# Two-block transformer kernel: the gated product turned by VectorE in squares of 32 instead of by TensorE

## What is computed

```
def swiglu(x, w_gate, w_up, w_down):
    return (jax.nn.silu(x @ w_gate) * (x @ w_up)) @ w_down

h = h + 0.5 * swiglu(rms_norm(h, norm_ffn), w_gate, w_up, w_down)   # eight times, 1024 -> 2816 -> 1024
```

## Time and profile before

| | us |
|---|---|
| median of 3 runs | 1971.68 (1971.55 to 1972.51) |
| the profiled execution, its own time | 1972.77 |
| its span in the profile | 1971.0 |
| TensorE busy in the span | 1960.5 |
| VectorE busy | 1199.4 |
| ScalarE busy | 1018.6 |

### The profile page before, as it was taken

How to read it: one execution, slowest core, us unless ns; L and a number is a source line. 1 busy time by engine, 2 the same in 40 slices (tenths; PEclk the granted TensorE clock), 3 DMA queues, 4 the chain that set the end, 5 groups by cost and what they waited for, 6 DMA issues and landing times.

```text
span 1971.0 us, 26229 instructions
## 1 busy us (share of the span) xinstructions
PE 1960.5 (99%) x9838; PEld 1652.8 (84%) x9838; DVE 1199.4 (61%) x1817; ACT 1018.6 (52%) x1590; POOL 68.9 (3%) x77
## 2 busy tenths in 40 slices
PE   9999999999999999999999999999999999999999
PEld 7888988888888898888888898888888888888887
DVE  6555656556655566555755566655576555876554
ACT  6444555445554665444544447544475444755442
POOL 0100300000000000000000000000010000200000
PEclk9999999999999999999999999999999999999999
DMA  9655436553655426555555434555446553306550
GB/s 339 210 202 174 150 108 214 192 191 130 221 184 178 144 77 212 192 192 171 188 181 186 162 138 139 203 192 192 171 163 234 183 189 128 108 24 212 192 192 22
DMA packets 241050, 338.91 MB, mean 172 GB/s; under 512 B 5728, under 2 KB 206351, under 8 KB 240831
## 3 DMA queue, kind: packets, MB, share of 16 engines
q1 hardware_dynamic: 239710, 335.84, 50.5%
q0 software_dynamic: 496, 1.23, 0.2%
q10 hardware_dynamic: 752, 0.61, 0.1%
HBM read 336.61 MB, written 1.05 MB: 171 GB/s over the span
## 4 chain that ended last, share of the span: by engine, by line
PE 95%; DVE 2%; ACT 2%; DMA 1%; issue 0%; SPq 0%; POOL 0%; ACTq 0%
PE A L535 11%; PE A L537 11%; PE A L536 11%; PE G L535 10%; PE G L537 10%; PE G L536 10%; PE X L535 8%; PE X L537 8%; PE X L536 8%; PE A L1226 1%; PE A L904 1%; PE G L964 1%; PE X L964 1%; PE X L1210 1%; PE G L1238 1%; DVE wl L496 0%
## 5 line engine op out<-in xcount | busy, mean ns | idle before, releaser
L496 DVE TENSOR_TENSOR wl<-raw,wh 128x1024 fp32r<-128x1024 f32 (+1 forms) x553 | 653.8, 1221 | 121.3 <-ACT wh L487 120.3
L487 ACT ACTIVATE wh<-raw 128x1024 fp32r<-128x1024 f32 (+1 forms) x553 | 561.9, 1058 | 144.1 <-PE A L537 102.6
L535 PE MATMUL G<-wh,xh 128*128 128x512 f32 (+1 forms) x814 | 322.1, 396 | 0.2
L537 PE MATMUL G<-wh,xl 128*128 128x512 f32 (+1 forms) x814 | 317.2, 390 | 0.0
L536 PE MATMUL G<-wl,xh 128*128 128x512 f32 (+1 forms) x814 | 316.3, 389 | 0.0
L535 PE MATMUL X<-wh,xh 128*128 128x512 f32 x672 | 265.8, 395 | 0.3 <-DVE wl L496 0.3
L537 PE MATMUL X<-wh,xl 128*128 128x512 f32 x672 | 262.3, 390 | 0.0
L536 PE MATMUL X<-wl,xh 128*128 128x512 f32 x672 | 261.6, 389 | 0.0
L537 PEld LDWEIGHTS G<-wh,xl 128*128 128x128 f32 x814 | 152.8, 188 | 32.3
L535 PEld LDWEIGHTS G<-wh,xh 128*128 128x128 f32 x814 | 152.9, 188 | 30.9 <-DVE xl L2399 0.6
L536 PEld LDWEIGHTS G<-wl,xh 128*128 128x128 f32 x814 | 153.1, 188 | 29.9
(11 more groups left out here) (487 smaller groups left out, 2787.5 us busy)
## 6 DMA issues: line engine op xcount, KB each, us to landing
raw<-in_ffn_w_in SPq DMA_DIRECT2D x88, 1024.0 KB, 6.8
raw<-in_ffn_w_down SPq DMA_DIRECT2D x44, 1024.0 KB, 6.5
raw<-in_ffn_w_out SPq DMA_DIRECT2D x44, 1024.0 KB, 7.1
raw<-in_ffn_w_gate SPq DMA_DIRECT2D x42, 1024.0 KB, 5.5
raw<-in_ffn_w_up SPq DMA_DIRECT2D x42, 1024.0 KB, 7.5
raw<-in_a_w_in SPq DMA_DIRECT2D x12, 1024.0 KB, 6.1
raw<-in_ab_w_in SPq DMA_DIRECT2D x8, 1024.0 KB, 6.8
raw<-in_kv_w SPq DMA_DIRECT2D x6, 1024.0 KB, 6.5
```

The lines of the kernel that those rows point to most:

```text
L487: nc.scalar.activation(hi, r, ACT.Copy).then_inc(hi_done[u], 1)
L496: nc.vector.tensor_tensor(lo, r, hi.bitcast(F32), ALU.subtract).then_inc(lo_done[u], 1)
L535: nc.tensor.matmul(o, sh, rh, start=start, stop=False)
L537: return nc.tensor.matmul(o, sl, rh, start=False, stop=stop)
```

## The change

`turn_hid` goes out of TensorE's step for the blocks 0 to 9 of each phase. In its place VectorE's `turn_squares` turns the product in SBUF, right behind `hidden`: a VectorE transpose turns squares of 32 by 32. Sixteen of them, one for each pair of input and output groups of 32 partitions, put each square in its place of the 128 by 128 transpose; each takes the squares of both token tiles and both halves of the 256 columns at once. `hid_hi` and `hid_lo` then read SBUF (`hid_t`) in place of PSUM. The last block of each phase is still turned by TensorE (`turn_hid`, `last_hid_hi`, `last_hid_lo`). ScalarE computes Silu in one pass, so `hidden` has one product per token tile in place of two, and `rstd2` is gone. Four events of the mixers are merged into two, with the counts moved accordingly.

```diff
@@ TensorE
-                def turn_hid(b, turn=None):
-                    at = 0 if turn is None else 4 * turn
+                def turn_hid(b):
                     for t in range(NT):
-                        pe.wait_ge(hid_done, 2 * (FFN_BLOCKS * f + b) + t + 1 + at)
+                        pe.wait_ge(hid_done, 2 * (FFN_BLOCKS * f + b) + t + 1)
...
                 def step(b, turn=None):
                     gate_up(b, 0, turn)
-                    turn_hid(b - 1, turn)
                     gate_up(b, 1, turn)
                     down(b - 1, turn)
...
                 gate_up(end, 0)
-                turn_hid(end - 1)
                 gate_up(end, 1)
@@ ScalarE
-                        A_(sig[:, t, :], GB[b % 2][t][:, 0:S], ACT.Sigmoid, scale=rstd[:, t:t + 1]).then_inc(sig_ready, 1)
+                        A_(sig[:, t, :], GB[b % 2][t][:, 0:S], ACT.Silu, scale=rstd[:, t:t + 1]).then_inc(sig_ready, 1)
...
                 def hid_hi(b, turn=None):
-                    at = 0 if turn is None else 4 * turn
+                    at = 0 if turn is None else 2 * turn
+                    act.wait_ge(squares_turned, (FFN_BLOCKS - 1) * f + b + 1 + at)
                     for t in range(NT):
-                        act.wait_ge(hid_turned, 2 * (FFN_BLOCKS * f + b) + t + 1 + at)
+                        A_(hidh[:, b % 2, t * S:(t + 1) * S], hid_t[:, t, :], ACT.Copy).then_inc(hidh_done, 1)
+
+                def last_hid_hi():
+                    b = FFN_BLOCKS - 1
+                    for t in range(NT):
+                        act.wait_ge(hid_turned, 2 * f + t + 1)
                         A_(hidh[:, b % 2, t * S:(t + 1) * S], GB[b % 2][t][:, 0:S], ACT.Copy).then_inc(hidh_done, 1)
...
             act.wait_ge(dve_chain, 1)
-            A_(zinv[:, 0:1], y[:, 0, 0:1], ACT.Sigmoid)
+            A_(zinv[:, 0:1], y[:, 0, 0:1], ACT.Silu)
@@ VectorE
                         dve.wait_ge(sig_ready, n + t + 1)
-                        V.tensor_tensor(gated[:, t, :], GB[b % 2][t][:, 0:S], sig[:, t, :], ALU.mult).then_inc(gated_done, 1)
-                    for t in range(NT):
-                        dve.wait_ge(gated_done, n + t + 1)
-                        V.scalar_tensor_tensor(hid[:, t, :], GB[b % 2][t][:, S:2 * S], rstd2[:, t:t + 1], gated[:, t, :],
+                        V.scalar_tensor_tensor(hid[:, t, :], GB[b % 2][t][:, S:2 * S], rstd[:, t:t + 1], sig[:, t, :],
                                                ALU.mult, ALU.mult).then_inc(hid_done, 1)
+
+                def turn_squares(b, turn=None):
+
+                    at = 0 if turn is None else 4 * turn
+                    dve.wait_ge(hid_done, 2 * (FFN_BLOCKS * f + b) + 2 + at)
+                    for q in range(4):
+                        for g in range(4):
+                            src = hid[32 * q:32 * (q + 1), :, :].rearrange("p t (c g j) -> p t c g j", c=2, g=4)
+                            dst = hid_t[32 * g:32 * (g + 1), :, :].rearrange("p t (c q j) -> p t c q j", c=2, q=4)
+                            last = V.transpose(dst[:, :, :, q, :], src[:, :, :, g, :])
+                    last.then_inc(squares_turned, 1)
...
                     hidden(b - 1, turn)
+                    turn_squares(b - 1, turn)
                     for half in downs:
                         prep(name, half, (2,))
                     for u in (0, 1):
...
-                link(V.tensor_tensor(rstd2, rstd, rstd, ALU.mult))
```

More of the change, by code:

```diff
@@ L346, in blocks_program @@
         mhf, mlf = mh[:].rearrange("p c n -> p (c n)"), ml[:].rearrange("p c n -> p (c n)")
-        sumsq, meansq, rstd, rstd2 = stat(2), stat(2), stat(2), stat(2)
+        sumsq, meansq, rstd = stat(2), stat(2), stat(2)
         zinv = stat(4)
@@ L354, in blocks_program @@
         sig = cut(work, 0, 2, S)
-        gated, hid = cut(work, 2 * S, 2, S), cut(work, 4 * S, 2, S)
+        hid = cut(work, 2 * S, 2, S)
+        hid_t = cut(work, 4 * S, 2, S)
         PT = cut(work, 0, 2, TRI)
@@ L375, in blocks_program @@
         xhi_done, xlo_done, acc_done = sem("xhi_done"), sem("xlo_done"), sem("acc_done")
-        sig_ready, gated_done, hid_done = sem("sig_ready"), sem("gated_done"), sem("hid_done")
+        sig_ready, hid_done = sem("sig_ready"), sem("hid_done")
+        squares_turned = sem("squares_turned")
         hid_turned, hidh_done, hidl_done = sem("hid_turned"), sem("hidh_done"), sem("hidl_done")
@@ L1861, in ffn @@
                     prep(name, FT + 1, (0, 1))
-                hid_hi(FFN_BLOCKS - 1)
+                last_hid_hi()
             def start(name):
@@ L1954, in fox_mixer @@
                 link(A_(fox["e"], fox["nz"], ACT.Exp))
-                A_(fox["e"], fox["e"], ACT.Ln, bias=1.0).then_inc(event("fox_ln"), 1)
+                A_(fox["e"], fox["e"], ACT.Ln, bias=1.0).then_inc(event("gate_ln"), 1)
                 for g in range(4):
@@ L1961, in fox_mixer @@
                     last = A_(decay[at:at + FOX_H, :], A[3][at:at + FOX_H, 0:S], ACT.Copy, scale=-1.0)
-                last.then_inc(event("fox_sums_hi"), 1)
+                last.then_inc(event("gate_hi"), 1)
                 wait_half(act, "fox", *ROWS["fox"][1][:2])
@@ L2067, in mlstm_mixer @@
                 link(A_(mls["e"], mls["nz"], ACT.Exp))
-                A_(mls["e"], mls["e"], ACT.Ln, bias=1.0).then_inc(event("ml_ln"), 1)
+                A_(mls["e"], mls["e"], ACT.Ln, bias=1.0).then_inc(event("gate_ln"), 1)
                 prep("mlstm", 3)
@@ L2072, in mlstm_mixer @@
                     last = A_(decay[at:at + ML_H, :], mls["top"][at:at + ML_H, 0, P:], ACT.Copy, scale=-1.0)
-                last.then_inc(event("ml_top_hi"), 1)
+                last.then_inc(event("gate_hi"), 1)
                 def gates(chunks):
@@ L2460, in hid_lo, with last_hid_lo @@
                         dve.wait_ge(hidh_done, 2 * (FFN_BLOCKS * f + b) + t + 1 + at)
+                        part = slice(t * S, (t + 1) * S)
+                        V.tensor_tensor(hidl[:, b % 2, part], hid_t[:, t, :], hidh[:, b % 2, part].bitcast(F32),
+                                        ALU.subtract).then_inc(hidl_done, 1)
+                def last_hid_lo():
+                    b = FFN_BLOCKS - 1
+                    for t in range(NT):
+                        dve.wait_ge(hidh_done, 2 * (FFN_BLOCKS * f + b) + t + 1)
                         part = slice(t * S, (t + 1) * S)
@@ L2527, in ffn @@
                     prep(name, FT + 1, (0, 1))
-                hid_lo(FFN_BLOCKS - 1)
+                last_hid_lo()
                 if name == "ffn0":
@@ L2650, in fox_mixer @@
                 split_keys(1)
-                dve.wait_ge(event("fox_ln"), 1)
+                dve.wait_ge(event("gate_ln"), 1)
                 V.scalar_tensor_tensor(fox["logf"], fox["z"], 0.0, fox["e"], ALU.min, ALU.subtract
@@ L2658, in fox_mixer @@
                                            ).then_inc(o_lo, 1)
-                dve.wait_ge(event("fox_sums_hi"), 1)
+                dve.wait_ge(event("gate_hi"), 1)
                 V.scalar_tensor_tensor(decay[32:40, :], A[3][32:40, 0:S], -1.0, decay[32:40, :].bitcast(F32),
@@ L2801, in mlstm_mixer @@
                 prep("mlstm", 2)
-                dve.wait_ge(event("ml_ln"), 1)
+                dve.wait_ge(event("gate_ln"), 2)
                 V.scalar_tensor_tensor(mls["logf"], z[:, :, 8:16], 0.0, mls["e"], ALU.min, ALU.subtract
@@ L2830, in mlstm_mixer @@
                                 ).then_inc(event("ml_top_out"), 1)
-                dve.wait_ge(event("ml_top_hi"), 1)
+                dve.wait_ge(event("gate_hi"), 2)
                 V.scalar_tensor_tensor(decay[32:40, :], top[32:40, 0, P:], -1.0, decay[32:40, :].bitcast(F32), ALU.mult,
```

## The result

The changed kernel takes 1981.57 us (median of 5 runs, 1980.83 to 1984.31); the kernel before took 1972.28 beside it on the same chip (5 runs, 1971.55 to 1973.58). The ratio is 1.005, with a 95% interval of 1.0035 to 1.0064: **slower by 9.3 us**, about 0.5%. The forecast was 1971.2, no difference. The time lies inside the range, but the chance for slower was 0.37, and the likeliest case was another one.

A forecast was written before the change was run, and what follows sets the result against it. TensorE, busy 1960.5 of 1971.0 us, was taken as the bound. Transposes saved (-38.4), waits (+36.6) and a table load (+1.3) summed to -0.5 us: 1972.3 in the profiled execution, 1971.2 as median; range 1954 to 1986.

The forecast's parts named there:

- Granted clock 1.00 after each wait: Expected sign in the trace: TensorE keeps its full granted clock after every wait at a phase start.
- The granted clock falls in the waits: Rival: 1.2 GHz for half a block after each of eight waits, +43 us at most, half giving 1993; chance 0.08.
- TensorE's gain: Each of 80 blocks loses TensorE's four transposes, 0.48 us each time, 38.4 us off.
- The transposes: On VectorE, one transpose takes p = 0.33 us without overlap; T, the time of all sixteen, is 5.28 us.
- overlap: Rival: VectorE transposes in a row overlap, 0.20 to 0.23 us each, -20 to -15 us, 1952 to 1957; chance 0.11.
- a slow element and of VectorE as the bound: Rival: two cycles per 4-byte element, 0.43 us per transpose, make VectorE bound every block, 1993 us; chance 0.10.
- the one that named 1980: Rival: each VectorE transpose takes between 0.36 and 0.42 us, +5 to +14 us, 1980 us; chance 0.10.
- The waits: TensorE's lateness at eight phase starts and ffn2's block 3: 9T - 11.34 + 0.4 = 36.6 us.
- ffn6: Second half of block 1: TensorE late by T - 1.26 us; kv's second table load falls in ScalarE's idle time, free.
- ffn2, block 3: After the rotary tables' angles: TensorE late by T - 2.48, plus about 0.4 us for a later last hidl.
- The kv load ahead of the gates: ScalarE needs one new table load before the kv stage's Sigmoid gates, on the chain, +1.3 us.
- the middle blocks inside their cover: In the other blocks VectorE's residuals come 4.7 us later, within 6.34 us before TensorE needs them: no cost.

The follow-up runs named there:

- the filled kernel: Changed kernel plus TensorE matmuls whose results nobody reads, placed where TensorE would wait at the phase starts: 1967.13 us, ratio 0.9973 to the kernel before.
- the kernel without waits: Changed kernel, but block 0 of each phase is turned by TensorE as before, the other nine by VectorE: 1937.59 us, ratio 0.9822.
- kernel with Silu gates: Against the kernel with TensorE's turn in all first blocks: the two kv gates use Silu instead of Sigmoid, without VectorE's product: 1937.9 us, ratio 0.9822.
- the mixed kernel: Changed kernel with squares behind the second half's residuals, block 1's hidl before the down residuals, and TensorE turning ffn0's block 0: 1939.95 us, ratio 0.9835.

## Why the prediction was wrong

**The step that failed** is this one under "What would show it": "Granted clock 1.00 after each wait". The sum holds waits, and after each wait TensorE at its old pace. It has no term for the clock; that stood only as a rival, "The granted clock falls in the waits", at 0.08, and its two prices (43 at most, half of it taken) were both too high for what happened: seven of the eight starts, 8 to 13 matmuls each, 13.8 us by the ledger and 14.4 by the filled kernel. Without it the changed kernel is faster by 5.5 us. The argument for 0.08 was that before, with 10.5 us of idle time in all, the clock stays up. But those idle times were short ones: behind the first matmul of the program the profile has none longer than this one in the last mixer, 0.76:

```profile
1705.39 0.44 PE L1664 MATMUL A<-const,arena 128*128 128x128 f32 x2 [0.76 <-POOL arena L858]
```

They said nothing of a single wait of 3.8. The Trainium skill (TensorE: Matmul & The Clock Gate, "Why this matters for your kernels") advises against idle gaps of more than about 3 us, and the forecast's waits were all above that; the trace agrees in seven of eight, and the two waits of 2.5 and the one of 2.2 in the experiments show that less can do it.

**TensorE's gain**: 0.48 forecast, 0.49 measured, 80 times; right, and shown by itself in the kernel without waits.

**The transposes**: p = 0.33 forecast, 0.316 measured:

```profile
L2467 DVE STREAM_TRANSPOSE work<-work x1280: 299/303/311, 24.8 to 1954.7; 32x128 f32<-32x128 f32 x183
```

303 ns and a gap of 13 to 14, T = 5.05. The duration lies between the two rows that bounded it, somewhat below their middle of 316, and the hold that L2816's pair showed is the one found here, also 14 ns. The rivals of overlap, of a slow element and of VectorE as the bound are out. So is the one that named 1980, next to the measured 1981.6: it had p from 0.36 to 0.42, and its number is near by luck.

**The waits**, at T = 5.05: 9 x 5.05 - 11.34 + 0.4 = 34.5 by the formula, 33.7 measured. Seven starts come out within 0.3. Two terms are off, and hide each other:
- ffn6: 3.79 by the formula, 5.17 measured. The second table load of the kv stage, costed at nothing since it "falls in ScalarE's idle time before the first Silu", comes on demand, behind the gate product, and holds that Silu back:

```profile
1494.77 1.28 ACT L1793 ACT_TABLE_LOAD   x1 [1.53 <-PE G L539]
1496.07 0.84 ACT L1793 ACTIVATE work<-G,st 128x256 f32<-128x256 f32 x2
```

- ffn2, block 3: 2.97 by the formula, 0.30 measured. Before, Sin needed a table of its own and both ways back cost loads; after, Sin and Silu are in one table. The trace of before has 21 table loads, that of after 17, none for Sin, although Silu and the kv gates now differ; the kernel with Silu alone has 17 too. ScalarE around the two Sin, the loads before and the rows after:

```profile
510.98 1.28 ACT L1849 ACT_TABLE_LOAD   x1
...
515.22 1.28 ACT L487 ACT_TABLE_LOAD   x1
...
518.54 1.28 ACT L1794 ACT_TABLE_LOAD   x1
...
519.21 0.21 ACT L1855 ACTIVATE st<-arena 128x32 f32<-128x32 f32 x1
519.33 1.99 ACT L489 ACTIVATE wh<-raw 128x1024 fp32r<-128x1024 f32 x2
521.23 0.82 ACT L1793 ACTIVATE work<-G,st 128x256 f32<-128x256 f32 x2
```

VectorE's last operation of the angles and the residuals behind it, before and after: 514.64 to 517.61, a distance of 2.97, and 518.86 to 520.41, 1.55. That is 1.42 less; 0.38 is an idle time ahead of `hidden` that is gone; and the `hidl` ahead of the angles came 0.45 sooner against TensorE, not 0.4 later, since it no longer waits for TensorE's turn.

**The kv load ahead of the gates**: 1.3 forecast, 0 measured. The load is there,

```profile
1471.56 1.06 ACT L489 ACTIVATE wh<-raw 128x1024 fp32r<-128x1024 f32 x1 [1.87 <-DMA raw<-in_ffn_w_in]
1472.64 1.28 ACT L2195 ACT_TABLE_LOAD   x1
```

but the transfer that ScalarE waits for ahead of it landed 1.4 us earlier against TensorE than before, and the two cancel. Why it landed earlier was not tried. The kernel with Silu gates, which has no such load, is no faster than the one with TensorE's turn in all first blocks alone (1937.9 against 1937.59), which agrees.

**Silu** at no cost, and the middle blocks inside their cover: right.

Two prices of rivals are misadded, and neither touches the forecast: by the sum's own terms p from 0.36 to 0.42 gives +4 to +12, not +5 to +14, and p = 0.295 with the 0.4 gone gives about -6.0, not -5.6.

So the terms forecast sum to -5.5 instead of -0.5, and the missing one is +13.8.

## What to carry to other kernels

When work is moved from the bound engine to another one, price the middle of a phase and its start apart: here nine tenths of the gain came for nothing, and all of the loss at the first block, where nothing lay ahead to cover it. Leaving the first block with TensorE, or ordering what the next consumer reads ahead of the moved work, turns +9 us into -35 or -32. And a wait of TensorE of more than 2 us is to be priced above its length: with the matmuls behind it at 1.2 GHz, a wait of 3.8 cost 5.4 in three phases, 6.2 in a fourth and only its own length in a fifth, and one of 5.2 cost 7.6 to 7.8; the page's clock digits don't show it, so look at the distance of matmul starts behind the wait.

## What the runs showed of the hardware

- The granted clock, inside the phases: it fell to the 1.2 GHz level after waits of 3.8 to 6.2 us in all places but one, after both of 2.5, after one of 2.2 and not after another of 2.26, and after none of 1.67. The exception is ffn2's 3.76 in the changed kernel, the same length as four that lowered it; with 4.73 it fell there too. In some places it was down at the first matmul, in others some 1.5 us later (ffn1: start at 310.75, pace of 0.43 from 312.33). In the first 11 us of the program it was down behind shorter waits as well: six matmuls 0.43 apart after a wait of 1.60 in the mixed kernel and after one of 1.64 in the kernel with Silu alone (granted clock 0.50 in both), none after one of 1.03 in the kernel with TensorE's turn in all first blocks. Length alone doesn't decide, and what else does is open; the advice of 2 us above comes from waits inside the phases.
- Two VectorE transposes in a row overlap by 63 to 72 ns when they write the same 32 partitions, and stand 13 to 14 ns apart when they write others; this held 1200 times in the changed kernel. The Trainium skill (VectorE: DVE Perf Modes, "Two Vector instructions with no wait between them") has such a hold; these runs agree and add its size.
- A fp32 transpose of 32 partitions by 128 elements takes 303 ns on VectorE, one of 64 elements 232 to 245 ns at the head of a pair.
- Sin and Silu share a table of ScalarE: no load stood between them (17 loads in all); Sin and Sigmoid didn't, with a load of 1283 ns ahead of Sin and two behind it (21 in all).
